# One of four channel chunks of a depthwise convolution moved from VectorE to TensorE, and projections that wait for their input chunk by chunk

## The reference: what is computed

```
xn = rmsnorm(x);  q, k, v, val, gate = split(xn @ w_in)
A  = sliding-window attention(q, k, v)            # 8 heads of 64, window 128
u  = val * sigmoid(gate)                          # 512 channels
C  = silu(layernorm(depthwise_conv(u, 31 taps) + b)) @ pw
h  = x + concat(rmsnorm(A), rmsnorm(C)) @ w_out
y  = h + PEER(rmsnorm(h))                         # top-k retrieval of 16384 one-neuron experts
```

## Time and profile before

| | |
|---|---|
| time, median of 3 runs | 1882.97 us (1882.95 to 1884.08) |
| the profiled execution | 1883.62 us, of which the span of the trace is 1881.8 us |
| PE busy | 1644.2 us (87%) |
| DVE busy | 1461.3 us (78%) |
| ACT busy | 753.2 us (40%) |
| POOL busy | 543.1 us (29%) |

### The profile page before, as it was taken

One profiled execution on the slowest core, in us unless ns is written; L12 is line 12 of the kernel. 1 busy time (PEld: TensorE's weight loads), 2 busy tenths in 40 slices (PEclk: granted clock), 3 DMA queues, 4 the chain that ended last, 5 costly groups with the idle time before them and its releaser, 6 DMA issues.

```text
span 1881.8 us, 22921 instructions
## 1 busy us (share of the span) xinstructions
PE 1644.2 (87%) x8237; PEld 1437.2 (76%) x8237; DVE 1461.3 (78%) x2718; ACT 753.2 (40%) x1243; POOL 543.1 (29%) x395
## 2 busy tenths in 40 slices
PE   6877436997699999899899899889999999999997
PEld 4755325776598778899799899889778778777876
DVE  2558784326876999877799999995779888988986
ACT  2112211312243222444588788875333333333332
POOL 0000000000011333211356656663334443443430
PEclk8988756998799999999899999999999999999999
DMA  5110500124356787777699999999999999999995
GB/s 184 49 34 12 65 1 0 40 79 135 102 162 211 288 291 233 245 231 240 200 370 386 403 399 369 390 390 390 361 348 390 362 364 396 366 366 372 391 351 185
DMA packets 164359, 477.43 MB, mean 254 GB/s; under 512 B 28063, under 2 KB 61535, under 8 KB 162071
## 3 DMA queue, kind: packets, MB, share of 16 engines
q1 hardware_dynamic: 108951, 274.63, 42.0%
q0 software_dynamic: 55296, 201.35, 28.5%
HBM read 420.93 MB, written 54.42 MB: 253 GB/s over the span
## 4 chain that ended last, share of the span: by engine, by line
PE 56%; DVE 31%; issue 5%; DMA 3%; ACT 3%; SPq 1%; DVEq 0%; ACTq 0%
PE ps L758 23%; PE ps L686 16%; PE ps L517 8%; DVE ring L1315 6%; DVE cacc L1421 5%; DVE lo L1200 3%; PE ps L736 3%; DMA gelu_matrix<-gest 2%; DVE tsi L1212 2%; DVE tsi L1215 2%; PE ps L529 2%; DVE sm L1213 2%; DVE acc L1319 2%; DVE gA L1362 1%; DVE gB L1362 1%
## 5 line engine op out<-in xcount | busy, mean ns | idle before, releaser
L1028 POOL DMA_INDIRECT ring<-in_u,idx x192 | 273.5, 1424 | 936.4 <-DVE ijg L1295 552.5
L1200 DVE TENSOR_TENSOR lo<-raw,hi 128x1024 fp32r<-128x1024 f32 x256 | 313.1, 1223 | 140.0 <-ACT hi L887 134.5
L887 ACT ACTIVATE hi<-raw 128x1024 fp32r<-128x1024 f32 x256 | 270.3, 1056 | 319.7 <-PE ps L758 316.1
L686 PE MATMUL ps<-xh,hi 128*128 128x384 f32 x1024 | 356.5, 348 | 27.0 <-DVE lo L1200 26.8
L1028 POOL DMA_INDIRECT ring<-in_v,idx x192 | 268.2, 1397 | 363.4 <-DVE acc L1319 345.9
L686 PE MATMUL ps<-xl,hi 128*128 128x384 f32 x1024 | 348.3, 340 | 0.0
L686 PE MATMUL ps<-xh,lo 128*128 128x384 f32 x1024 | 347.6, 339 | 0.0
L758 PE MATMUL ps<-hi,ah 128*128 128x512 f32 x768 | 238.7, 392 | 22.2 <-DVE al L1392 22.1
L1319 DVE SCALAR_TENSOR_TENSOR acc<-ring,hu,acc 128x1024 f32<-128x1024 f32 x192 | 245.4, 1278 | 1.6
L758 PE MATMUL ps<-lo,ah 128*128 128x512 f32 x768 | 237.8, 391 | 0.0
L758 PE MATMUL ps<-hi,al 128*128 128x512 f32 x768 | 237.2, 390 | 0.0
(11 more groups left out here) (170 smaller groups left out, 1951.9 us busy)
## 6 DMA issues: line engine op xcount, KB each, us to landing
raw<-in_uT SPq DMA_DIRECT2D x128, 512.0 KB
raw<-in_v SPq DMA_DIRECT2D x128, 512.0 KB
wring<-in_wblk SPq DMA_DIRECT2D x48, 512.0 KB
gelu_matrix<-gest SPq DMA_DIRECT2D x64, 384.0 KB
gate_matrix<-Gs SPq DMA_DIRECT2D x16, 1536.0 KB
Gl<-gate_matrix SPq DMA_DIRECT2D x128, 192.0 KB
gel<-gelu_matrix SPq DMA_DIRECT2D x128, 192.0 KB
wring<-in_wblk SPq DMA_DIRECT2D x16, 256.0 KB
```

The lines of the kernel that those rows point to most:

```text
L686: mm = nc.tensor.matmul(out, a[:, n % 2, w], b[:, c, :], start=(c == 0 and k == 0), stop=(c == DC - 1 and k == 2))
L887: nc.scalar.activation(hi[:, s % 2, :], raw[:, s % RAWS, :], ACT.Copy).then_inc(s_hi, 1)
L1028: pool.indirect_dma_start(ring[:, r % SLOTS, :], None, table, bass.IndirectOffsetOnAxis(idx[:, t, c:c + 1], 0)).then_inc(g_in[r % SLOTS], 16)
L1200: nc.vector.tensor_tensor(lo[:, s % 2, :], raw[:, s % RAWS, :], hi[:, s % 2, :].bitcast(F32), ALU.subtract).then_inc(s_lo, 1)
```

## The change

Chunk 3 of the convolution is taken from DVE. ACT makes 31 diagonal 128x128 matrices `taps[:, j, :]` (the identity times tap j's weight of each channel), eight ahead of the squares of K, Q0 and Q1 and seven ahead of those of Q2. In units 4 to 7, PE runs two matmuls for each tap, `taps[:, j, :]` against the shifted 512 prompt columns and the shifted 64 sample columns, four taps after S and four (in unit 7 three) after PT, all summed in PSUM pair 0. After the sample attention, DVE adds the bias and writes `cacc`. `CONV_AT` puts the 12 quarters left on DVE one to a slot, in slots 2 to 13; before, slots 2 and 5 had two. Besides, five waits for a whole array become waits for one chunk at a time: `K` on `xn`, `woa0` and `wob0` on `mg`, `pw` on the Silu, `wqa0` on the second `xn`.

```diff
-CONV_AT = [0, 0, 0, 2, 3, 4, 6, 7, 8, 9, 10, 11, 12, 13, 14, 15, 16]
+CONV_AT = [0, 0, 0, 1, 2, 3, 4, 5, 6, 7, 8, 9, 10, 11, 12, 12, 12]
+TAPS_AT = [0, 4, 8, 12, 16, 20, 24, 28, TAPS]
@@ psum_plan
+    plan += [("taps", 0)]
@@ PE
-            def gemm(name, rhs, kc=DC, cut=0, last=True):
+            def gemm(name, rhs, kc=DC, cut=0, last=True, made=None, base=0):
...
                 for k in range(kc):
+                    if made is not None:
+                        pe.wait_ge(made, base + k + 1)
...
-            pe.wait_ge(s_xn, DC)
-            gemm("K", xn)
+            gemm("K", xn, made=s_xn)
...
+            def conv_taps(i):
+                c = CC - 1
+                if i == 0:
+                    take("taps")
+                    pe.wait_ge(s_glu, 2 * c + 2)
+                    pe.wait_ge(s_tap, TAPS)
+                    pe.wait_ge(s_stpad, 16)
+                    pe.wait_ge(s_pz, 1)
+                pair, _ = use["taps"]
+                for j in range(TAPS_AT[i], TAPS_AT[i + 1]):
+                    ends = dict(start=(j == 0), stop=(j == TAPS - 1))
+                    nc.tensor.matmul(ps[pair][:, 0:SEQ], taps[:, j, :], gpad[:, c, j:j + SEQ], **ends)
+                    mm = nc.tensor.matmul(ps[pair][:, SEQ:T], taps[:, j, :], spad[:, c, :, j:j + DS], **ends)
+                if i == 7:
+                    mm.then_inc(R[pair], 1)
...
                 if u < CC:
                     gemm(f"glu{2 * u}", xn)
+                else:
+                    conv_taps(2 * (u - CC))
...
                 if u < CC:
                     gemm(f"glu{2 * u + 1}", xn)
+                else:
+                    conv_taps(2 * (u - CC) + 1)
...
-            pe.wait_ge(s_mg, CC)
-            gemm("woa0", attn_half, kc=CC)
+            gemm("woa0", attn_half, kc=CC, made=s_mg)
...
-            pe.wait_ge(s_sw, CC)
-                gemm(f"pw{m}", cacc, kc=CC, cut=(m % 2) * CC, last=(m % 2 == 1))
+                gemm(f"pw{m}", cacc, kc=CC, cut=(m % 2) * CC, last=(m % 2 == 1), made=s_sw)
...
-            pe.wait_ge(s_mg, 2 * CC)
-            gemm("wob0", conv_half, kc=CC)
+            gemm("wob0", conv_half, kc=CC, made=s_mg, base=CC)
...
-            pe.wait_ge(s_xn2, DC)
+                    if name == "wqa0":
+                        pe.wait_ge(s_xn2, k + 1)
@@ ACT
+            act.wait_ge(s_ct, 64)
             for i, name in enumerate(["K", "Q0", "Q1", "Q2", "Q3"]):
+                for j in range(8 * i, min(8 * i + 8, TAPS)):
+                    nc.scalar.activation(taps[:, j, :], ident[:, :], ACT.Copy,
+                                         scale=col("cw", (CC - 1) * TAPS + j)).then_inc(s_tap, 1)
@@ DVE
+            p = ready("taps")
+            nc.vector.tensor_scalar(cacc[:, CC - 1, :], p[:, 0:T], col("cb", CC - 1), None,
+                                    ALU.add).then_inc(s_conv_d, 1)
             rstd("msA")
```

More of the change, by code:

```diff
@@ L233, in hymba_peer @@
             spad = mb("spad", [P, CC, NDB, PAD + DS])
+            taps = mb("taps", [P, TAPS, P])
             on1024 = mb("on1024", [P, P])
@@ L301, in hymba_peer @@
         s_conv_d = sem("conv_by_dve")
+        s_tap = sem("tap_weights_ready")
         s_nm = sem("negmax_ready")
@@ L1156, in attn_added @@
                 ins.then_inc(free, 1)
+            p = ready("taps")
+            nc.vector.tensor_scalar(cacc[:, CC - 1, :], p[:, 0:T], col("cb", CC - 1), None,
+                                    ALU.add).then_inc(s_conv_d, 1)
+            dve.wait_ge(s_conv_d, CC)
+            dve.sem_inc(F[use["taps"][0]], 1)
             rstd("msA")
```

## The result

| | before | after |
|---|---|---|
| time, median of 4 runs each on one chip | 1883.53 us (1882.95 to 1884.29) | 1856.18 us (1849.64 to 1860.24) |
| ratio, 95% interval | | 0.985 (0.982 to 0.988) |
| the profiled execution | 1883.62 us | 1858.78 us |

The forecast was 1858.4 us. First the page of after: span and busy time.

The account below looks back on a forecast made before the run. DVE, filled by the convolution, was taken to set the pace from 250 to 300 us while PE idles. Attention -10.6, first norm -5.2, merge -5.0, second norm -4.4: -25.2 from 1883.6 gives 1858.4 us; 8-in-10 range 1847 to 1869.

Parts of the forecast that it names:

- A tap on PE: Units 4 to 7: each tap's 512-column and 64-column matmuls on PE were taken as 1.09 us at full clock.
- The fourth rival: PE taps: weight loads are not hidden, so units 4 to 6 and unit 7 cost more; 1865 us, chance 0.05.
- Units 4 to 6: Second halves of these units: PE takes over from DVE, with 2.3 us clock loss in each; +6.1 us together.
- the first rival: Attention units: the clock mostly holds, giving -19 us in place of -10.6; time 1850 us, chance 0.22.
- The third rival: Second halves of units 2 to 7 and three early starts: PE stays at 1.2 GHz; 1899 us, chance 0.04.
- Unit 1: Attention unit 1: slot 2 loses eight DVE taps ahead of the division, transposes wait less; -9.3 us (-10.8 to -7.9).
- Unit 7: Last attention unit: from 24.03 to 17.1 us with three PE taps in its second half; -6.9 us (-8.1 to -0.3).
- The diagonals: ACT's 31 diagonals, 0.391 us each, are hidden behind PE's next projections; otherwise 3.1 us in each of four steps.
- The norms: First and second norm: projections start after one chunk of `xn`; -5.2 us and -4.4 us.
- The second rival: Both norms: PE starts earlier at half clock and only stays there longer, gaining nothing; 1868 us, chance 0.11.
- The merge: After the sample attention: `woa0` starts after one of four chunks, so `pw0` starts earlier; -5.0 us (-1.2 at worst).
- after 350 us the stages are not edited: After 350 us: the mixer's stages follow each other without overlap, so what they gain reaches the end.

Follow-up runs that it names:

- experiment 3: After, with all of a unit's eight PE taps ahead of the transposes and none behind: 1856.37 us, ratio 0.982 to before.
- experiment 1: After, with the waits for whole arrays put back, so the convolution part alone: 1874.71 us, ratio 0.991 to before.
- experiment 2: Before, with only the waits for single chunks (waits alone), the whole convolution on DVE: 1877.61 us, ratio 0.995 to before.
- experiment 5: After, with all of a unit's PE taps behind the transposes and none ahead: 1874.66 us, ratio 0.995 to before.
- after with the filler: After, plus three spare 512-column matmuls in each of the last loop's seven PE pauses: 1853.49 us, ratio 0.982 to before.
- before with the filler: Before, plus three spare 512-column matmuls in each of the last loop's seven PE pauses: 1883.03 us, ratio 0.998 to before.
- experiment 7: Before and after, each with three spare matmuls in each of the last loop's seven pauses: 1883.03 and 1853.49 us.
- the split: After, with all eight PE taps ahead of the transposes in units 4 to 6, four and three in unit 7: 1857.11 us, ratio 0.982 to before.

## Why the prediction was right

**The forecast held, and its mechanisms with it.** A tap costs DVE time only where DVE's slot is the later one, and PE time where PE is the later engine: in the second halves, and, as experiment 3 showed, in the first half of unit 7 once seven taps stand there. Experiments 1 and 2 show the two halves of the change at -15.6 and -12.7 us, with -10.6 and -14.6 forecast; the one is larger and the other smaller, and that the sum came so near the forecast is in part luck. Experiments 3 and 5 show on which side of the transposes a PE tap costs: none there, 4.9 us less; all there, 17.4 more.

**A tap on PE.** 3 taps from 200.55 to 203.80 are 1.083 us each, for the 1.09 taken. The parts differ: 0.915 for the 512 columns (0.862 forecast) and 0.17 for the 64 (0.226 taken, half of it the bound). The fourth rival, weight loads that are not hidden, falls. The Trainium skill's rule ("TensorE: Matmul & The Clock Gate", Part 3, "What overlaps and what doesn't") would have made a tap an estimated 1.5 us (1.09 and 0.43 for the loads); the trace does not agree, with its 1.083.

**Units 4 to 6, a term slightly mis-sized.** The clock's loss was put at 2.3 us in each second half. In units 4 and 5 the transposes lose 0.9 (1.97 for 1.09) and the four taps, 4.80 us against 4 x 1.083, 0.5: 1.35. In unit 6 the taps take 6.36 and the loss is 2.9. So these halves last 9.5, 9.6 and 11.1 for the 10.5 forecast, +5.0 for +6.1. The granted clock in unit 6:

```profile
245.00:250.00 5.00, 4.94 (x14) 3.39 (x15) 4.82 (x12) 1.02 (x1) 0.00 (x0) 0.50 0.00 0
```

The clock rises behind the transposes, within the first tap (unit 4, 1.38 us for its prompt part) or after two (unit 6, above): between the forecast and the first rival, as the attention part is (-14.7, for -10.6 and -19). The third rival, half clock throughout, is refuted by these rows.

**Unit 1** took the best end of its range: the transposes no longer wait until the clock is lost (0.66 us for four, 1.11 before), and the second half is 10.3 us.

**Unit 0** was costed at nothing and gives 1.5, which differs from execution to execution. Its first half is 11.1 us (12.5 before) with the same work in it, a projection that runs longer or shorter at half clock. The twelve profiles have two lengths of this unit: 21.2 to 21.7 us in nine, 22.7 to 22.9 in three (before, waits alone, after with the filler). The kernel before with the filler, whose code is that of before up to the last loop and whose S starts as late, is among the short ones:

```profile
87.84 2.07 PE L566 MATMUL ps<-kT,qT 64*128 64x128 f32 x8 [5.97 <-DVE qS L1073]
...
109.42 1.16 PE L566 MATMUL ps<-kT,qT 64*128 64x128 f32 x8 [0.83 <-DVEq L1118]
```

These are 21.58 us. So neither the edit nor an earlier S is what makes the unit shorter.

**Unit 7.** Forecast 17.1, measured 17.62: first half 9.0 for 8.85, second half 8.6 for 8.25.

**The diagonals** are hidden, and cheaper than the 0.391 us taken: eight in 2.43 us, and the square of the projection behind them follows at once while PE is in its next projection (trace of after, in order of time):

```profile
41.16 2.43 ACT L816 ACTIVATE taps<-ident_sb,cols_sb 128x128 f32<-128x128 f32 x8
43.50 0.63 ACT L821 ACTIVATE sq<-ps 128x576 f32<-128x576 f32 x1
...
48.02 1.13 PE L535 MATMUL ps<-sq,onblk 128*128 128x288 f32 x4
```

**The norms.** K started 0.97 us after DVE started the first chunk, at 21.61 for the 22.03 forecast, and the scores 4.5 us sooner. That S of unit 0 came just the 5.2 us earlier is partly luck: 0.65 of it lie ahead of the first chunk. From the first chunk to S it is 62.15 us for 66.71, 4.6 less (4.8 in experiment 2); but the versions that wait for all 8 chunks in the two other profiles (experiment 1, and before with the filler) have 67.95 and 67.77, so the edit is worth 4.6 to 6.1. The second rival, that an early start at half clock buys nothing, is refuted by experiment 2. **The merge** gave 4.0 for 5.0: `var` ends 3.8 us sooner after the reciprocal as forecast (12.75 for 16.57), but the means ahead of it ran longer, at half clock:

```profile
297.27 6.63 PE ps L535 x16
```

**A step that did not hold: "after 350 us the stages are not edited", so that what is gained reaches the end.** (Taken by the letter the first half is wrong too: `wqa0`, whose wait is edited, starts at 438, and the prediction itself counts it.) In the profiled execution 3.8 us were given back: the dense stage after the ranking is 2.0 shorter and the last loop 5.8 longer. Nothing ties this to the change: in the twelve profiles the stage from the ranking to the last loop, the same code in all, lasts 872.0 to 878.9 us. After, unaltered, ran the loop in 543.3 us in another profile with two falls of the clock, and in 551.5 with five; with no falls, before and after differ by 1.7 (experiment 7). In the profiled after, the five falls cost 7.9 us by the times of their groups, before's one 1.6; the pauses sum to 20.2 us in after and to 19.1 in before. (In part this is offset at the loop's start, where before ran at half clock and after did not.) So the profiled execution was this close to the forecast by luck: the gain was 3.4 us larger than forecast up to the ranking, and 3.8 were lost behind it.

The Trainium skill ("TensorE: Matmul & The Clock Gate", Part 1, "What's actually happening") says that the same kernel shows different numbers of slow matmuls from run to run, and that the ramp costs less than 1% of a typical span. On the first these runs agree: two profiles of after have five and two falls in the last loop. On the second they show only that loop, where the five falls of after cost 7.9 us and the five of the split 10.6, 0.4% and 0.6% of the span. But this is as much as the parts of the change that were to be told apart.

**Open:** why, of two pauses of the last loop that are equally long, one is followed by half clock and the other is not; what makes the pauses of the loop longer in one execution than in another; what spreads the filled kernels' runs by another 4.6 to 8.5 us (the stage between the ranking and the loop was not filled); and why unit 0 has two lengths.

## What to carry to other kernels

Work moved to an idle engine gains only where the engine it leaves sets the end, and costs where the engine it joins does: place it by halves of the step. In the last step, where the engine it leaves has no such work any more, look anew: seven taps ahead of the transposes cost time there, and neither split tried came under the 17.6 us of after. Where a consumer takes its input chunk by chunk, let it wait chunk by chunk: here 12.7 us at the ranking for a few waits, 11.6 without what lay ahead of the edit, even in the second norm, where PE's step at half clock (0.65 us, from the prediction's rows) is a little shorter than DVE's 0.74. If a loop has short recurring pauses of TensorE, look at the granted clock behind each before comparing versions that differ by less than the spread; a few spare matmuls in the pause may be worth more than the next edit, and one too many costs about its full length: with four in place of three the loop took 5.2 to 6.5 us more.

## What was not expected of the hardware

- A matmul of 64 float32 columns behind a load of 128x128 weights takes 0.17 us at full clock, of 512 columns 0.91 to 0.92.
- ACT scales a 128x128 identity by a column in 0.30 us each (eight in 2.43), where scaled copies in a later stage took 0.391.
- Pauses of PE of 2.0 to 3.2 us are sometimes followed by half clock and sometimes not, at the same place of the same program. One that was, a little longer, in the loop of after, in order of time:

```profile
1362.89 0.70 PE L782 MATMUL ps<-hi,ah 128*128 128x512 f32 x2 [3.76 <-DVE al L1425]
```

The stretch from there (length, PE busy, granted clock, DMA share, GB/s): PE resumes at full clock and falls to half within it.

```profile
1363.00:1366.00 3.00, 3.00 (x9) 0.64 0.87 298
```

- Three spare matmuls at each of seven pauses narrowed the runs of the kernel before from 16.0 to 6.9 us, with a small gain in its median (1886.63 to 1883.03, ratio 0.996 to 1.000).
